# Four wide products, then four narrow ones: the order of TensorE's matmuls in the feature passes of a two-block transformer kernel

## What is computed

```
h2 = rmsnorm(x, g_norm2) * (1.0 + scale2) + shift2
x = x + gate2 * (jnp.square(jax.nn.relu(h2 @ w_mlp1)) @ w_mlp2)
...
def swiglu(x, w_gu, w_down):
    g, u = jnp.split(x @ w_gu, 2, axis=-1)
    return (jax.nn.silu(g) * u) @ w_down
...
x = layer_norm(DEEPNORM_ALPHA * x + 0.5 * swiglu(x, ffn_w_gu[i, 0], ffn_w_down[i, 0]), ...)
...
x = layer_norm(DEEPNORM_ALPHA * x + y, ln_g[i, 1], ln_b[i, 1])     # y: attention times its output matrix
...
x = layer_norm(DEEPNORM_ALPHA * x + 0.5 * swiglu(x, ffn_w_gu[i, 1], ffn_w_down[i, 1]), ...)
```

## Time and profile before

| | |
|---|---|
| median of 3 runs | 1342.78 us (1342.57 to 1343.0) |
| the profiled execution's own time | 1342.86 us |
| its span, first to last instruction | 1341.1 us |
| granted TensorE clock, mean | 0.997 |
| PE busy | 1319.9 us, 98% of the span, 6741 matmuls |
| DVE, ACT, POOL busy | 65%, 52%, 6% |
| H matmuls (line 846), L matmuls (line 848) | 1344, 1344 |

### The profile page before, as it was taken

One profiled execution on the slowest core, in us unless ns is written; L12 is line 12 of the kernel. 1 busy time (PEld: TensorE's weight loads), 2 busy tenths in 40 slices (PEclk: granted clock), 3 DMA queues, 4 the chain that ended last, 5 costly groups with the idle time before them and its releaser, 6 DMA issues.

```text
span 1341.1 us, 17337 instructions
## 1 busy us (share of the span) xinstructions
PE 1319.9 (98%) x6741; PEld 1109.8 (83%) x6741; DVE 876.1 (65%) x1210; ACT 696.8 (52%) x1112; POOL 77.1 (6%) x114
## 2 busy tenths in 40 slices
PE   7999999999999999999999999999999999999997
PEld 5788877888888888888877888888888888888885
DVE  5787668777666665665447664676654676766464
ACT  3765564454444554555665553555554544555452
POOL 1401101000002000001001000001000010100000
PEclk9999999999999999999999999999999999999999
DMA  9867744557555655656516556556645565665651
GB/s 350 321 208 243 283 176 158 188 212 259 188 203 189 205 189 183 200 176 227 188 63 219 190 188 209 190 178 217 211 179 182 188 220 188 208 199 189 196 175 69
DMA packets 160222, 268.45 MB, mean 200 GB/s; under 512 B 9755, under 2 KB 103052, under 8 KB 160012
## 3 DMA queue, kind: packets, MB, share of 16 engines
q1 hardware_dynamic: 152428, 239.47, 52.4%
q0 software_dynamic: 7648, 27.85, 6.0%
q10 hardware_dynamic: 64, 0.02, 0.0%
HBM read 266.21 MB, written 1.07 MB: 199 GB/s over the span
## 4 chain that ended last, share of the span: by engine, by line
PE 95%; DVE 2%; ACT 1%; DMA 1%; issue 0%; SPq 0%; POOL 0%; DVEq 0%; ACTq 0%; POOLq 0%
PE TBB L846 12%; PE UPP L846 12%; PE Y L791 10%; PE Y L793 10%; PE Y L792 10%; PE UPP L791 7%; PE UPP L793 7%; PE UPP L792 7%; PE UPP L848 6%; PE TBB L848 6%; PE TBB L892 2%; PE UPP L1010 1%; PE Y L924 1%; PE Y L931 1%; PE Y L1010 1%; DMA WADA<-in_w_ada 0%
## 5 line engine op out<-in xcount | busy, mean ns | idle before, releaser
L1734 DVE TENSOR_TENSOR WL<-RAW,WH 128x1024 fp32r<-128x1024 f32 (+1 forms) x434 | 499.1, 1196 | 167.5 <-ACT WH L1317 163.8
L1317 ACT CAST WH<-RAW 128x1024 fp32r<-128x1024 f32 (+1 forms) x434 | 421.7, 1028 | 194.1 <-PE Y L793 74.8
L846 PE MATMUL UPP<-AHL,WH 128*128 128x512 f32 x672 | 215.7, 397 | 0.0
L846 PE MATMUL TBB<-AHL,WH 128*128 128x512 f32 x672 | 211.1, 395 | 0.0
L791 PE MATMUL Y<-WH,HH 128*128 128x512 f32 (+1 forms) x496 | 192.0, 387 | 0.0
L792 PE MATMUL Y<-WL,HH 128*128 128x512 f32 (+1 forms) x496 | 191.4, 386 | 0.0
L793 PE MATMUL Y<-WH,HL 128*128 128x512 f32 (+1 forms) x496 | 191.3, 386 | 0.0
L791 PE MATMUL UPP<-WH,AHL 128*128 128x512 f32 x432 | 176.8, 409 | 1.0 <-DVE AHL L1740 0.5
L793 PE MATMUL UPP<-WH,AHL 128*128 128x512 f32 x432 | 169.0, 391 | 0.0
L792 PE MATMUL UPP<-WL,AHL 128*128 128x512 f32 x432 | 168.4, 390 | 0.0
L848 PEld LDWEIGHTS TBB<-AHL,WL 128*128 128x128 f32 x672 | 126.3, 188 | 29.8
(11 more groups left out here) (260 smaller groups left out, 1385.0 us busy)
## 6 DMA issues: line engine op xcount, KB each, us to landing
RAW<-in_ffn_w_gu SPq DMA_DIRECT2D x176, 512.0 KB, 4.9
RAW<-in_ffn_w_down SPq DMA_DIRECT2D x80, 512.0 KB, 4.3
RAW<-in_w_mlp SPq DMA_DIRECT2D x64, 512.0 KB, 4.4
RAW<-in_w_in SPq DMA_DIRECT2D x34, 512.0 KB, 5.9
PIECE<-in_w_ada POOLq DMA_DIRECT2D x32, 512.0 KB, 5.9
RAW<-in_a_w_in SPq DMA_DIRECT2D x24, 512.0 KB, 4.7
WADA<-in_w_ada SPq DMA_DIRECT2D x14, 512.0 KB, 9.4
RAW<-in_w_out SPq DMA_DIRECT2D x8, 512.0 KB, 4.2
```

Source lines behind the costliest of these rows:

```text
L846: pe.matmul(banks[:, block, :], WH[:, u % 2, cols[block]], AHL[:, k, :], start=k == 0, stop=False)
L1317: act.copy(WH[:, u % 2, q * n:(q + 1) * n], raw_half(u, q // 2)[:, (q % 2) * n:(q % 2 + 1) * n]).then_inc(wh_done, 1)
L1734: ve.tensor_tensor(WL[:, u % 2, o], raw_half(u, q // 2)[:, (q % 2) * n:(q % 2 + 1) * n], WH[:, u % 2, o].bitcast(F32), ALU.subtract).then_ ...
```

## The change

It has three parts.

1. In `feature`, two k-tiles are taken together: H of both k-tiles and both blocks (four matmuls of 512 columns), then L of both (four of 256). Where the blocks are apart, it is two H and two L of one block.
2. In the last tile of the last unit, all k-tiles of half 0 come ahead of those of half 1. The last matmul of half 0 counts a new semaphore, `half_done`, and the last layer norm's first DVE instruction waits for that alone.
3. The first quarter of unit ("aout", 1) is made by ACT ahead of its last two `my_high`, and by DVE ahead of its last two `my_low`; the other three quarters stay behind them.

```diff
-                order = [(k, block) for k in range(kts) for block in range(2)]
-                if inner is not None:
-                    order.sort(key=lambda kb: kb[1])
-                steps = [(k, (block,)) for k, block in order] if inner is not None else [(k, (0, 1)) for k in range(kts)]
-                for k, blocks in steps:
...
+                together = 2
+                spans = [range(k, k + together) for k in range(0, kts, together)]
+                if inner is None:
+                    steps = [(ks, (0, 1)) for ks in spans]
+                else:
+                    steps = [(ks, (block,)) for block in range(2) for ks in spans]
...
+                for ks, blocks in steps:
+                    for k in ks:
+                        for block in blocks:
...
+                            quarters(u, part, (k + 1) * width)
+                            pe.matmul(banks[:, block, :], WH[:, u % 2, columns(k, block)], AHL[:, k, :],
+                                      start=k == 0, stop=False)
+                    for k in ks:
+                        for block in blocks:
+                            mm = pe.matmul(banks[:, block, 256:512], WL[:, u % 2, columns(k, block)], AH[:, k, :],
+                                           start=False, stop=k == kts - 1)
+                        if blocks[-1]:
+                            quarter_taken(mm, u, part, (k + 1) * width)
...
+                closing = (u, tok) == (len(UNITS) - 1, 1)
+                steps = [(k, h) for k in ks for h in range(2)]
+                if closing:
+                    steps.sort(key=lambda kh: kh[1])
...
+                    elif (k, h) == (kts - 1, 0):
+                        mm.then_inc(half_done, 1)
...
+            round_unit(UNIT[("aout", 1)], (0,))
             for tok in range(TOK):
                 my_high(tok, 1)
-            round_unit(UNIT[("aout", 1)])
+            round_unit(UNIT[("aout", 1)], (1, 2, 3))
...
                     for h in range(2):
+                        if h or turned or tok == 0:
+                            ve.wait_ge(mm_done, MM_NO[UNIT[unit], tok])
+                        else:
+                            ve.wait_ge(half_done, 1)
...
+            split_unit(UNIT[("aout", 1)], (0,))
             my_low(1)
-            split_unit(UNIT[("aout", 1)])
+            split_unit(UNIT[("aout", 1)], (1, 2, 3))
```

More of the change, by code:

```diff
@@ L445, in build @@
         out_ready = sem("out_ready")
+        half_done = sem("half_done")
         out_done = sem("out_done")
@@ new lines, in feature, with columns @@
+                together = 2
[4 more added lines that the diff above has]
+                    steps = [(ks, (block,)) for block in range(2) for ks in spans]
+                def columns(k, block):
+                    col = k * width + (2 * P * block + P * part if key[0] == "gu" else P * (2 * part + block))
+                    return slice(col, col + P)
@@ new lines, in feature @@
+                for ks, blocks in steps:
+                    for k in ks:
+                        for block in blocks:
+                            if k == 0:
+                                if block and inner is not None:
+                                    from_tmp(*inner)
+                                if FEATURE_NO[key] % 2:
+                                    pe.wait_ge(*turn_bank_free(TURNED_BEFORE[key][block]))
+                                else:
+                                    pe.wait_ge(*up_emptied[up_before[u, part][block]])
+                            quarters(u, part, (k + 1) * width)
[7 more added lines that the diff above has]
+                            quarter_taken(mm, u, part, (k + 1) * width)
@@ L864, in deep @@
                     pe.wait_ge(y_free[tok], DEEP[product])
[L865 to L873, removed]
+                closing = (u, tok) == (len(UNITS) - 1, 1)
+                steps = [(k, h) for k in ks for h in range(2)]
+                if closing:
+                    steps.sort(key=lambda kh: kh[1])
+                for k, h in steps:
+                    if turns and (k, h) == (2, 1):
+                        chain_turns(*turns)
+                    o = k * D + h * HALF
+                    quarters(u, tok, o + HALF)
+                    w = slice(o, o + HALF)
+                    mm = three(dst[h][:, :], ah[:, k0 + k, ts], al[:, k0 + k, ts], WH[:, u % 2, w],
+                               WL[:, u % 2, w], first and k == 0, last and k == kts - 1)
+                    if not closing:
                         quarter_taken(mm, u, tok, o + HALF)
+                    elif (k, h) == (kts - 1, 0):
+                        mm.then_inc(half_done, 1)
                 if ks[-1] == kts - 1:
@@ L2158, in begin @@
                 def begin(tok):
-                    ve.wait_ge(mm_done, MM_NO[UNIT[unit], tok])
                     for h in range(2):
+                        if h or turned or tok == 0:
+                            ve.wait_ge(mm_done, MM_NO[UNIT[unit], tok])
+                        else:
+                            ve.wait_ge(half_done, 1)
                         s = slice(h * HALF, (h + 1) * HALF)
```

## The result

The changed kernel took 1345.11 us (median of 20 runs), the kernel before 1342.82 (20 runs beside them): a ratio of 1.0016, 95% interval 1.001 to 1.0022. It is slower, by 2.3 us. The profiled execution's span is 1343.4 us at a mean granted clock of 0.997; before it was 1341.1 at the same clock, so the clock has no part in this.

What follows compares the result with a forecast made beforehand. The prediction took the kernel to be bound by PE, as a queue of matmuls. Gains of 1.6 (feature order), 0.61 (tail) and 0.8 us (output quarter) summed to 3.0, giving 1339.8 us by the median, range 1338.9 to 1344.1.

Steps and rivals of the forecast that it cites:

- What bounds the kernel: Whole kernel: PE busy 1319.9 of 1341.1 us, a queue of matmuls; closer starts, fewer stalls or shorter head and tail help.
- steady sum of 1386.8 ns: Feature passes: four H at 226.7 and four L at 120 ns, the time of two k-tiles (an eight) without width-change losses.
- Part 1: Feature passes: taking two k-tiles together wins 1.6 us, bounds 0 and -2.4.
- short form: Four H restarting behind L matmuls in 0.91 us, at most 10 ns above four steady ones; forecast case, chance 0.50.
- bound of 0 on the losing side: Feature passes: at worst the new order costs what it costs now, so no loss.
- long form: Four H restarting behind L matmuls in 0.93 us, 23 ns above four steady ones.
- long restart: Rival, feature passes: every run of four H starts slowly, 1.40 us an eight; kernel 1343.9 or 1345 us; chance 0.18.
- rival by which an eight loses the same 6.3 ns: Feature passes: order of widths has no effect, only the other parts win, 1341.4 us; chance 0.27.
- Part 2: Kernel's tail: half 0's sum hides behind the last 12 matmuls, winning 0.61 us.
- Part 3: Output unit ("aout", 1): its first-quarter stall of 0.45 us goes, and the next load starts some 0.8 us earlier.
- term of 0.8: Gain of the early output quarter, through a shorter wait at norm c3's transposes: 0.8 us, bounds 0 and 1.47.
- The sum: Whole kernel: 1.6 + 0.61 + 0.8 = 3.0 us won, giving 1339.8 us by the median.

Runs made afterwards that it cites:

- e3: Kernel before, with feed-forward blocks in different run orders (four or eight k-tiles together, two together, single H then L); eights 1396.7, 1391.7, 1403.3, and 1386.7 or 1413.2 ns.
- e1: Kernel before with only the new order of the feature passes (two k-tiles together): 1346.05 us, ratio 1.0024.
- e8: Kernel before with only the last tile's halves apart, feature order and first quarter as before: 1342.12 us, ratio 0.9992.
- e2: Changed kernel with the feature passes put back to one k-tile together, the two other parts kept: 1341.86 us, ratio 0.9993.
- e9: Kernel with single products (H, then its L), each pass begun by 0 to 3 k-tiles in one run; eights 1399.4 to 1413.2 ns, no kernel time given.
- e10: e2 with single products (H, then its L) in all feature passes and one HHHHLLLL lead-in where a stretch begins: 1345.24 us, ratio 1.0017.

## Why the prediction was wrong

**What bounds the kernel** was right: a queue of matmuls, in which distances between starts count. The steady distances and the steady sum of 1386.8 ns held: e3's good kind of "single" runs at 1386.7. No stretch came out below that sum by more than 0.2 ns an eight.

**Part 1 is the step that failed**, and with it direction and range. I wrote "with the short form an eight takes between 1.38 and 1.39 us ... I take 1.389", -1.6 us, bounds 0 and -2.4. Measured: 1403.3 ns, 10.0 more than before, 316 x 10.0 = 3.2 us. The passes with their blocks together did lose 3.0, as near the ends of a stretch an eight loses less than 10; those with their blocks apart won 0.08 us, where 0.3 was forecast for their slow pairs; all stretches together +2.9. The bound of 0 on the losing side was wrong too, though the earlier trace rows had shown a dearer restart. Two sentences carried the choice, and both fell:

- "An eight of today has two restarts of H and loses 6.3 ns in all, less than one long form costs", so I expected one restart an eight, at some 4 ns. But today's restarts are cheap, at 3.3 ns net: a run of two H pays 12.9 ns where a run of eight pays 27, and its two L bring back 9.7. Halving the number of restarts also doubled the runs, and took the net price from 3.3 to 16.5 ns. I had treated the price as a constant while the change altered the thing that it depends on.
- "A run of four H gives the stream room to settle". Settling is what costs: four H pay 22.3 of the 27 ns that a whole restart takes, and four L bring back only 5.8. Longer runs pay little more a return, and have fewer of them, but eight in a row are still dearer than the order of before (1396.7 against 1393.3 ns); only 16 come out below it (1391.7).

Both prices stood in the rows as "forms", short 0.91 and long 0.93 us, and I left it to chance which would come. In the changed kernel every run of four H inside a stretch takes the long one. The ends of today's stretches had shown how open it was: of the ten 512-column streams behind them, six start in the short form and four in the long one. The hint was in the earlier trace rows, pairs of 353.3 and 346.7 ns from one code: the cost depends on more than the number of changes.

**The rival "long restart"** is what happened. It put an eight at 1.40 us and the kernel at 1343.9, or 1345 with the rest of the long form; measured were 1.4033 and 1345.1. I gave it 0.18, as against 0.50 for the short form, on the argument above. The rival by which an eight loses the same 6.3 ns however the widths are arranged, with a chance of 0.27, is refuted by e1.

The Trainium skill ("TensorE: Matmul & The Clock Gate", Back-to-back issue gap) gives a gap by the columns for a lone matmul, and says that in a stream of loads and matmuls both set the spacing. By the runs a matmul's neighbours matter: the starts of 512-column matmuls lie 224 to 241 ns apart by what stood ahead of them (e3), around a steady 226.7.

**Part 2** was right in mechanism and size: 0.61 forecast, 0.61 in the trace, and e8 0.95 us in the medians with an interval that holds it.

**Part 3** was right in its first half. The stall is gone, and the load starts 1.0 us sooner against the attention's end where I had 0.8. The term of 0.8 was mis-sized, at 0.49 in these two traces (0.1 to 0.6 against all traces without part 3): I followed the chain back from X through DVE and ACT, and left POOL out of it, whose two instructions took 0.36 and 0.57 us in the trace of before. With ACT's casts earlier, DVE's two quarters run without a gap, and the variance is held to their end (in e3, without part 3, it was once held so too, for 2.18 us). I asked what is late next, and did not look for it on POOL. The Trainium skill ("SBUF — State Buffer", section "SBUF: two separate sides") states that a VectorE instruction with two SBUF inputs and a GpSimd one that reads SBUF contend for a shared pair of ports, which whichever starts first holds to its end. The trace agrees that the small instruction ends with VectorE's, at 715.30 and 715.22. Which of two waiting instructions comes next the runs do not settle: in the change and in e2 it was held over two of them in a row (2.39 us), in e1 over what was left of the first (1.05), and its next instruction over the second (1.39).

**The sum**: +2.9 (passes) - 0.61 - 0.49 = +1.8 in the trace, against +2.3 in the medians and in the spans. Another 0.28 comes from the ten 512-column streams behind the stretches: the first ten matmuls of each took 9 to 28 ns above steady before, 170 ns in all, and take 27 to 47 now, 445 in all. The last 0.2 comes in small steps outside the passes, and I have not placed it.

## What to carry to other kernels

The cost of a switch (of width here) isn't a constant to be multiplied by the number of switches: measure it at the run length that the new order will have, and if the trace has only other lengths, let the dearest one that it shows bound the range. Fewer switches paid only with runs of 16 matmuls a side, by 1.6 ns an eight; runs of eight were 3.4 ns dearer than those of two, and from two to four it was a loss of 3 us in 1343. Where a wait is shortened, follow the chain on all engines with the new times, the small GpSimd instructions beside VectorE's two-input work too. And where an engine's order also sets when the next loads start, moving its work can only move the wait: both reorderings of norm c3 removed a wait of 1.1 us, and PE was 0.75 and 1.06 us late at the third place of the table.

## What the runs showed of the hardware that was not expected

- A 512-column matmul behind a settled run of 256-column ones: starts at 233, 236, 228, 233, 231 ns, then the steady 227; about 27 ns above five steady ones. The 256-column ones behind 512: 114, 119, then 120, 7 ns below. The net 20 ns is the same in runs of 8 and 16; it is 16.5 in runs of 4 and 3.3 in runs of 2, where two H pay 12.9 ns and two L give back 9.7.
- H and L in strict alternation have at least two kinds that last over a whole stretch of some 300 matmuls, 1386.7 and 1413.2 ns an eight, from the same code (e3, e9, e10). The kind carries on from a pass of alternating H and L ahead, and a run of four H and four L between turned it in all five cases (e10). A third one, pairs of 230 + 117 ns, was seen in every second pass where each pass began with such a run (e9).
- A GpSimd instruction on one element a partition took from 0.30 to 2.39 us, by what VectorE ran beside it.
